# The first layer's MLP of a two-layer transformer block: its first matrix by seven half-size products in seven of eight blocks

## What is computed

```
def squared_relu_mlp(h, w_in, w_out):
    return jnp.square(jax.nn.relu(h @ w_in)) @ w_out
xl = xl + ml[5] * squared_relu_mlp(modulate(xl, norm_mlp_g[i], ml[3], ml[4]), w_mlp_in[i], w_mlp_out[i])
if not last:
    xc = xc + mc[5] * squared_relu_mlp(modulate(xc, norm_mlp_g[i], mc[3], mc[4]), w_mlp_in[i], w_mlp_out[i])
```

## Time and profile before

| | |
|---|---|
| median of 3 runs | 1614.97 us (1614.3 to 1968.04) |
| span of the profiled execution, first to last instruction | 1613.1 us |
| around the span in a run (median less span) | 1.9 us |
| PE busy in the span | 1595.3 us (99%) |
| DVE, POOL, ACT busy | 983.8 us (61%), 618.0 us (38%), 517.5 us (32%) |
| mean granted TensorE clock | 0.998 |

### The profile page before, as it was taken

The page is one execution under the profiler, slowest core; times in us unless marked ns, Lnnn a source line. Parts: engine busy times, 40 slices in busy tenths (PEclk is TensorE's granted clock), DMA queues, the critical chain, the costliest instruction groups (busy, mean ns, idle before and its releaser), DMA issues.

```text
span 1613.1 us, 24225 instructions
## 1 busy us (share of the span) xinstructions
PE 1595.3 (99%) x9440; PEld 1433.7 (89%) x9440; DVE 983.8 (61%) x1315; ACT 517.5 (32%) x931; POOL 618.0 (38%) x402
## 2 busy tenths in 40 slices
PE   8999999999999999999999999999999999999998
PEld 5889988989999999999999888878889888888887
DVE  5697457258756764865784678229975825344364
ACT  4422466233211211211211512138864422222222
POOL 2422565335323322432331544244505644444441
PEclk9999999999999999999999999999999999999999
DMA  9473212213252234223332122110002322323221
GB/s 361 181 284 134 92 41 99 92 66 105 77 185 80 77 122 140 100 95 117 105 112 97 66 91 92 65 56 1 1 1 89 107 93 92 104 91 99 96 79 53
DMA packets 50334, 162.99 MB, mean 101 GB/s; under 512 B 6336, under 2 KB 8768, under 8 KB 46656
## 3 DMA queue, kind: packets, MB, share of 16 engines
q1 hardware_dynamic: 50240, 161.68, 29.1%
HBM read 158.78 MB, written 2.10 MB: 100 GB/s over the span
## 4 chain that ended last, share of the span: by engine, by line
PE 93%; DVE 3%; DMA 2%; issue 1%; ACT 1%; SPq 0%; POOL 0%; POOLq 0%; DVEq 0%; ACTq 0%
PE ps L1714 26%; PE ps L1715 26%; PE ps L1716 26%; PE ps L2259 3%; PE ps L2221 2%; PE ps L2248 1%; PE ps L2126 1%; PE ps L2114 1%; PE ps L2154 1%; PE ps L1938 1%; DMA mod_late<-w_mod_dram 1%; DMA mod_big<-w_mod_dram 1%; DVE h L1315 1%; DMA raw<-units_dram 1%; PE ps L2149 1%
## 5 line engine op out<-in xcount | busy, mean ns | idle before, releaser
L625 POOL TENSOR_TENSOR w_lo<-raw,w_hi 128x1024 fp32r<-128x1024 f32 (+1 forms) x235 | 483.6, 2070 | 837.9 <-ACT w_hi L784 837.7
L1714 PE MATMUL ps<-h,w_hi 128*128 128x384 f32 (+2 forms) x1176 | 409.8, 348 | 1.7 <-DVE h L1315 1.2
L1715 PE MATMUL ps<-h,w_lo 128*128 128x384 f32 (+2 forms) x1176 | 407.6, 347 | 0.0
L1716 PE MATMUL ps<-h,w_hi 128*128 128x384 f32 (+2 forms) x1176 | 407.3, 346 | 0.0
L784 ACT ACTIVATE w_hi<-raw 128x1024 fp32r<-128x1024 f32 x187 | 197.8, 1058 | 372.7 <-PE ps L1716 366.1
L1714 PE MATMUL ps<-hid_lo,w_hi 128*128 128x384 f32 (+2 forms) x800 | 277.6, 347 | 0.0
L1715 PE MATMUL ps<-hid_hi,w_lo 128*128 128x384 f32 (+2 forms) x800 | 276.6, 346 | 0.0
L1716 PE MATMUL ps<-hid_hi,w_hi 128*128 128x384 f32 (+2 forms) x800 | 276.4, 346 | 0.0
L1714 PEld LDWEIGHTS ps<-h,w_hi 128*128 128x128 f32 x1176 | 221.3, 188 | 25.2 <-issue 3.4
L1716 PEld LDWEIGHTS ps<-h,w_hi 128*128 128x128 f32 x1176 | 221.2, 188 | 16.4
L1715 PEld LDWEIGHTS ps<-h,w_lo 128*128 128x128 f32 x1176 | 221.4, 188 | 16.0
(11 more groups left out here) (237 smaller groups left out, 2268.9 us busy)
## 6 DMA issues: line engine op xcount, KB each, us to landing
raw<-units_dram SPq DMA_DIRECT2D x187, 512.0 KB, 3.3
mod_ring<-w_mod_dram SPq DMA_DIRECT2D x96, 256.0 KB, 3.3
mod_big<-w_mod_dram SPq DMA_DIRECT2D x16, 1024.0 KB, 10.2
mod_late<-w_mod_dram SPq DMA_DIRECT2D x8, 1024.0 KB, 7.9
xl<-x_dram SPq DMA_DIRECT2D x2, 2048.0 KB, 8.4
bias<-bias_dram SPq DMA_DIRECT2D x8, 384.0 KB, 3.7
xc<-ctx_dram SPq DMA_DIRECT2D x2, 1024.0 KB, 10.5
out_dram<-out_t SPq DMA_DIRECT2D x16, 128.0 KB, 1.9
```

The lines of the kernel that those rows point to most:

```text
L625: ins = nc.gpsimd.tensor_tensor(w_lo[:, s, sl], raw[:, s, sl], w_hi[:, s, sl].bitcast(F32), op=ALU.subtract)
L1714: mm(out, a[0], b[1], start=start, stop=False)
L1715: mm(out, a[1], b[0], start=False, stop=False)
L1716: return mm(out, a[0], b[0], start=False, stop=stop)
```

## The change

MLP 0 gets 8 blocks of 512 hidden channels. Block 0 takes its first matrix as before (4 units, K of 1024). In blocks 1 to 7 the product of 1024 x 512 weights with 1024 x 768 rows is cut into halves along K, hidden channels and tokens (tokens 0 to 383 are `H0`, 384 to 767 `H1`) and is made of seven products of half size, in Winograd's form, in place of eight. One product is one unit of 24 matmuls with 384 columns. Four sums of weight quarters are made on POOL for each block (`w_sum`, `a21`, `a11`, L764 to L781), and four sums of token halves, which all blocks share, once on DVE (`t1f` to `t4f`, L1664 to L1672), ahead of and between the hidden rows of block 0. Products that belong together are summed in PSUM (`onto`), and between them ACT copies a partial sum of 128x768 to SBUF (`copy`, L979), and DVE adds PSUM to it (`joined`, L1721). Squares and parts are made by quarters of 128x768 (L1649 or L1647 on DVE, L983 on ACT, L1654 on DVE).

The second matrix sums over K of 512 in blocks 0 to 5 (each of their units has two output tiles of 24 matmuls), so the residual additions are made 8 times a block in 6 blocks; the last unit group sums over the 1024 channels of blocks 6 and 7. Units go from 64 to 85, loads stay 64. Modulation chunks move with the blocks: two in blocks 1 to 5, one in blocks 6 and 7; blocks 1 to 4 have a chunk with two instructions a step in the stretch of the products, and one with a single instruction in the stretch of the second matrix. The second layer's MLP stays.

The diff, cut to what is spoken of:

```diff
-STAGES = [("f", 4), ("q0", 4), ("k0", 4), ("dft", 3), ("v0", 4), ("out0", 8), ("mlp0", 64),
+STAGES = [("f", 4), ("q0", 4), ("k0", 4), ("dft", 3), ("v0", 4), ("out0", 8), ("mlp0", 85),
...
+def block_first(b):
+    return 0 if b == 0 else 8 + 11 * (b - 1) if b < 7 else 70
...
+                    def outer_sums():
+                        raw_here(1)
+                        raw_here(3)
+                        if b == 1:
+                            pool.wait_ge(t_lo, 4)
+                        else:
+                            pool.wait_ge(lo_made, M0 + block_first(b - 1) + 4)
+                        nc.gpsimd.tensor_tensor(w_sum[:], a21, a22, op=ALU.add).then_inc(w_sums, 1)
+                        raw_here(0)
+                        pool.wait_ge(w_sums, n + 1)
+                        nc.gpsimd.tensor_tensor(a21, a11, a21, op=ALU.subtract).then_inc(w_sums, 1)
+                    if b < 7:
+                        outer_sums()
+                    low(w)
+                    if b == 7:
+                        outer_sums()
+                    pool.wait_ge(w_sums, n + 2)
+                    pool.wait_ge(lo_made, w + 1)
+                    nc.gpsimd.tensor_tensor(a11, w_sum[:], a11, op=ALU.subtract).then_inc(w_sums, 1)
+                    low(w + 1)
+                    raw_here(2)
+                    pool.wait_ge(w_sums, n + 3)
+                    pool.wait_ge(lo_made, w + 2)
+                    nc.gpsimd.tensor_tensor(w_sum[:], a12, a11, op=ALU.subtract).then_inc(w_sums, 1)
+                    for j in range(2, 11 if b < 6 else 7):
+                        low(w + j)
...
+                def turn_high(j, dst, src):
+                    act.wait_ge(tf_made, (2, 3, 4, 1)[j])
+                    nc.scalar.activation(dst, src, ACT.Copy).then_inc(t_hi, 1)
+                for i in range(4):
+                    u = M0 + i
+                    act.wait_ge(unit_done, u + 1)
+                    for bank, c0, n in both if i < 3 else even:
+                        ins = nc.scalar.activation(hidl_f[:, i, c0:c0 + n], ps[:, 2 * pair_of(u, i, True) + bank, 0:n],
+                                                   ACT.Relu)
+                    ins.then_inc(relu0_made, 1)
+                    high_u(u + 4)
+                    act.wait_ge(sq0_made, i + 1)
+                    nc.scalar.activation(hidh[:, i], hidl_f[:, i], ACT.Copy).then_inc(hq_hi, 1)
+                    if i == 1:
+                        turn_high(0, t3h[:], t3f[:])
+                    elif i == 2:
+                        turn_high(1, t2h[:], t2f[:])
+                        turn_high(2, t4h[:], t4f[:])
+                act.wait_ge(unit_done, M0 + 4)
+                turn_high(3, h_hi[:, 0:4, H1], t1f[:])
...
+                next_block(1)
+                for b in range(1, BLOCKS):
+                    w, n = M0 + block_first(b), 4 * (b - 1)
+                    def copy(side, p, q, func=ACT.Copy):
+                        act.wait_ge(unit_done, w + p + 1)
+                        nc.scalar.activation(quarter(b, q)[2], part_ps(b, side), func).then_inc(s_copied, 1)
+                    def quarter_high(q):
+                        act.wait_ge(sq0_made, 4 * b + q + 1)
+                        nc.scalar.activation(quarter(b, q)[0], quarter(b, q)[2], ACT.Copy).then_inc(hq_hi, 1)
+                    high_sum(b, 3)
+                    copy(0, 0, 2)
+                    high_sum(b, 4)
+                    copy(1, 1, 1)
+                    high_u(w + 5)
+                    copy(0, 2, 0)
+                    high_u(w + 6)
+                    for q in range(4):
+                        if q == 3:
+                            copy(0, 6, 3, ACT.Relu)
+                        if b == 6 and q in (1, 2):
+                            high_sum(7, q)
+                        elif b != 6 or q == 0:
+                            high_u(w + 7 + q)
+                        quarter_high(q)
+                    if b < 6:
+                        next_block(b + 1)
...
+                def square(q, n, src):
+                    if n % 4 == 3 or n < 4:
+                        ins = tt(src, src, src, op=ALU.mult)
+                    else:
+                        ins = V.scalar_tensor_tensor(out=src, in0=src, scalar=0.0, in1=src, op0=ALU.max, op1=ALU.mult)
+                    ins.then_inc(sq0_made, 1)
+                def quarter_low(n, hi, lo, src):
+                    dve.wait_ge(hq_hi, n + 1)
+                    tt(lo, src, hi.bitcast(F32), op=ALU.subtract).then_inc(hq_made, 1)
+                def turn_low(j, lo, src, hi):
+                    dve.wait_ge(t_hi, j + 1)
+                    tt(lo, src, hi.bitcast(F32), op=ALU.subtract).then_inc(t_lo, 1)
...
+                def difference(dst, spare, j0, tok0, j1, tok1):
+                    tt(dst, half_f(j0, 0, tok0), half_f(j1, 0, tok1), op=ALU.subtract).then_inc(dsteps, 1)
+                    st.n = st.n + 1
+                    st.wait(tt(spare, half_f(j0, 1, tok0), half_f(j1, 1, tok1), op=ALU.subtract))
+                    tt(dst, dst, spare, op=ALU.add).then_inc(tf_made, 1)
+                def less(dst, src, n, j, tok):
+                    dve.wait_ge(tf_made, n)
+                    st.wait(tt(dst, half_f(j, 0, tok), src, op=ALU.subtract))
+                    tt(dst, dst, half_f(j, 1, tok), op=ALU.add).then_inc(tf_made, 1)
+                def first_square(i):
+                    dve.wait_ge(relu0_made, i + 1)
+                    square(i, i, hidl_f[:, i])
+                def first_low(i):
+                    quarter_low(i, hidh[:, i], hidl[:, i], hidl_f[:, i])
+                dve.wait_ge(h_made, step(1, 1, KT - 1) + 1)
+                difference(t1f[:], t4f[:], 0, H1, 0, H0)
+                first_square(0)
+                dve.wait_ge(tf_made, 1)
+                difference(t3f[:], t4f[:], 1, H1, 0, H1)
+                first_low(0)
+                less(t2f[:], t1f[:], 1, 1, H1)
+                first_square(1)
+                less(t4f[:], t2f[:], 3, 1, H0)
+                first_low(1)
+                turn_low(0, t3l[:], t3f[:], t3h[:])
+                first_square(2)
+                first_low(2)
+                turn_low(1, t2l[:], t2f[:], t2h[:])
+                turn_low(2, t4l[:], t4f[:], t4h[:])
+                first_square(3)
+                first_low(3)
+                turn_low(3, h_lo[:, 0:4, H1], t1f[:], h_hi[:, 0:4, H1])
+                def add_tile(b, m):
+                    w = M0 + block_first(b) + (7 if b else 4) + m // 2
+                    if m % 2:
+                        dve.wait_ge(unit_done, w + 1)
+                    else:
+                        dve.wait_ge(tile_done, 4 * b + m // 2 + 1)
+                    add_pieces(0, 2 + m % 2, m, 5, xa(0, b, m))
+                def steps(c, ks):
+                    for k in ks:
+                        mod_step(c, k)
+                for m in range(8):
+                    add_tile(0, m)
+                for b in range(1, BLOCKS):
+                    c = MOD_OF[b][0]
+                    def joined(side, p, q):
+                        dve.wait_ge(unit_done, M0 + block_first(b) + p + 1)
+                        dve.wait_ge(s_copied, 4 * (b - 1) + (3, 2, 1)[q])
+                        src = quarter(b, q)[2]
+                        tt(src, part_ps(b, side), src, op=ALU.add).then_inc(s_added, 1)
+                        dve.wait_ge(s_added, 3 * (b - 1) + q + 1)
+                        square(q, 4 * b + q, src)
+                    def low(q):
+                        quarter_low(4 * b + q, *quarter(b, q))
+                    steps(c, range(6))
+                    joined(1, 3, 0)
+                    steps(c, range(6, 7))
+                    low(0)
+                    joined(0, 4, 1)
+                    steps(c, range(7, 8))
+                    low(1)
+                    if b == 6:
+                        extract_late(c, 4)
+                    joined(1, 5, 2)
+                    low(2)
+                    dve.wait_ge(s_copied, 4 * b)
+                    square(3, 4 * b + 3, quarter(b, 3)[2])
+                    low(3)
+                    if b < 6:
+                        add_tile(b, 0)
+                        add_tile(b, 1)
+                        extract_late(c, 0)
+                        for m in range(2, 6):
+                            steps(c + 1, range(2 * m - 4, 2 * m - 2))
+                            add_tile(b, m)
+                        add_tile(b, 6)
+                        extract_late(c + 1, 0)
+                        add_tile(b, 7)
...
+            def first_mlp():
+                first_three(1, M0, [pair_of(M0 + j, j, True) for j in range(3)])
+                pe.wait_ge(relu0_made, 1)
+                unit(M0 + 3, (M0 + 3) % SLOTS, (M0 + 3) % 2, *h_t, even)
+                def second(b, before_tile):
+                    for n in range(4):
+                        u = M0 + block_first(b) + (7 if b else 4) + n
+                        s = u % SLOTS
```

(49 more changed lines are left out.)

405 lines of the change are left out of this document (271 added, 134 removed).

## The result

| | before | after |
|---|---|---|
| median, us | 1614.78 (1614.3 to 1968.04, 4 runs) | 1684.8 (1682.7 to 1684.93, 4 runs) |
| ratio | 1 | 1.0429, 95% interval 1.0414 to 1.0445 |
| span of the profiled execution, us | 1613.1 | 1683.0 |
| TensorE matmuls | 9440 | 9272 |

What follows compares the result with a forecast made beforehand. PE, busy 99% of the span, was taken as the bound. Span 1613.1 - 29.1 (saving) + 26.6 (block 0) + 40 (blocks 1 to 4) + 5 + 8 (last blocks) + 4.5 (clock) = 1668.1, plus 1.9: median 1670.0 us, range 1618 to 1704.

Steps and rivals of the forecast that it cites:

- The saving, -29.1: Blocks 1 to 7: seven products in place of eight save 168 matmuls on PE, 29.1 us.
- 64 instructions become 81 low parts: MLP 0: POOL's 64 instructions become 81 low parts and 28 weight sums, 15 in each block of 512.
- Block 0, +26.6 and 1.7 for the clock: Block 0 after unit 3: PE idles 26.6 us for DVE's ordered work, then loses 1.7 us at half clock.
- the bound was 18.2: Block 0: lower bound of PE's idle time, 18.2 us, if no DVE instruction meets POOL's.
- Blocks 1 to 4, +10 each and 0.7 for the clock: Blocks 1 to 4: PE waits 10 us a block for joined sums and quarters, plus 0.7 us each at half clock.
- Stalls at products 5 and 6: Blocks 1 to 4: PE waits for DVE's first and second `joined`, 1.7 and 0.5 us.
- cost at nothing: Second matrix's stretch, blocks 1 to 4: no loss, as PSUM reads cover DVE; otherwise tile 7 up to 3 us late.
- near 100% busy in the products' stretches: Sign to look for in blocks 1 to 4: DVE near 100% busy during the products.
- The clock, +4.5 in all: Half clock behind PE's waits: 1.7 us in block 0, 0.7 in each of blocks 1 to 4, 4.5 in all.
- Blocks 5 to 7, +13: Last blocks: late quarters cost 5 us in block 5; DVE's backlog from block 6 costs 8 us in block 7.
- DVE keeps up after block 0: Rival for the blocks after block 0: POOL's instructions fall into DVE's waits or PSUM reads, 1617 us; chance 0.21.
- DVE and POOL exclude each other almost wholly: Rival for blocks 1 to 4: hardly any POOL time is hidden, 18 us lost a block, 1702 us; chance 0.10.

Runs made afterwards that it cites:

- run 1: Changed kernel with POOL's low parts and weight sums, and ACT's copies of sums in `w_sum`, cut to 64 of 1024 columns: 1602.6 us.
- run 4: Changed kernel with PE's row sums of modulation chunk 10 moved from block 6 to behind product 1 of block 7: 1684.5 us, ratio 1.0437.
- run 9: Changed kernel with modulation sums in PSUM, block 0 and modulation work reordered, most squares on ACT, late-needed high parts postponed: 1596.9 us, ratio 0.9888.
- run 2: Changed kernel with seven of the eight steps of each late modulation chunk cut to 16 of 512 columns, POOL untouched: 1659.1 us.
- run 5: Changed kernel with the sums of the late modulation chunks kept in PSUM instead of SBUF, POOL's work and DVE's order unchanged: 1647.7 us.

## Why the forecast was right, and where it was off

The mechanism came as forecast: two waits in block 0 (20.25 and 2.97 us), waits for quarters' low parts in blocks 1 to 4, blocks of 75.6 us (74 forecast), and DVE's rows stretched while POOL works. The terms were less exact than their sum.

**The saving, -29.1.** Right: run 1 has blocks of 63.8 us, the counted time of 15 products' worth of matmuls and the row sums. (POOL's "64 instructions become 81 low parts" compares unlike counts: it is 64 and 85, since the page's count rises from 402 to 451, by 21 low parts and 28 sums. The 15 a block, which the sum uses, are right.) A 1536-wide instruction alone took 1.75 to 1.76 us, close to the 1.77 of the rows' slope.

**Block 0, +26.6 and 1.7 for the clock.** Right in size and mechanism: 27.9 together, 24.9 of waiting and 2.9 for the 17 matmuls at half clock behind it. The low part of unit 3 was forecast to end at 419.8 and ended at 418.13 (it starts at 417.17 and takes 0.96). All four of POOL's low parts met DVE, as said. Without meetings the bound was 18.2; run 1 has low part 3 end at 409.83, where PE would have needed it at 393.2, so 16.6 are the order's.

**Blocks 1 to 4, +10 each and 0.7 for the clock.** Measured 11.8 against 10.7. That the sum is so near is partly luck, as errors of both signs cancel. Stalls at products 5 and 6 (1.7 and 0.5) didn't come; quarters 1, 2 and 3 cost 3.0, 0.3 and 2.6 in block 2 (forecast 3.7, 0.7, 3.3). In exchange the second matrix's stretch, which I "cost at nothing", since PSUM reads are over half of it, had waits at tiles: 0.39 and 1.57 us in block 2, 1.85 and 0.63 in block 1. The split before tile 7 was late, as the bound of 3 us had allowed. And half clock adds 1.7 us in block 2 where 0.7 was forecast.

That DVE would be "near 100% busy in the products' stretches" nearly holds: 31.76 of 33.60 us in block 2, though over a whole block it is 64 of 75.7:

```profile
528.40:562.00 33.60, 30.53 (x175) 29.92 (x173) 31.76 (x28) 11.01 (x12) 18.62 (x7) 1.00 0.47 148
```

**The clock, +4.5 in all.** Too small. Counted by their starts, 103 matmuls of the stage run some 0.35 us apart and not 0.173, about 18 us together: 24 in block 0, 27 in block 1, 10 in each of blocks 2 to 4, 9 in block 5, 13 in block 6. Not all of it is lost: block 1, with 27 of them, takes 75.5 us, and block 2, with 10, takes 75.4, so a part only fills time in which PE would have waited for DVE. No run separates the two, and the clock's share of the miss stays open. Windows of 2 us in block 1 and block 2 (PE's busy time and count first, the clock third from the end):

```profile
486.00:488.00 2.00, 1.52 (x5) 1.52 (x6) 1.97 (x3) 0.00 (x0) 0.00 (x0) 0.50 0.59 215
...
562.00:564.00 2.00, 1.99 (x11) 1.99 (x12) 1.78 (x2) 0.15 (x1) 0.00 (x0) 1.00 0.39 152
...
568.00:570.00 2.00, 0.34 (x2) 0.34 (x3) 1.60 (x1) 0.00 (x0) 0.79 (x1) 1.00 0.11 29
570.00:572.00 2.00, 2.00 (x11) 2.00 (x10) 0.99 (x3) 0.00 (x0) 0.00 (x0) 0.78 0.61 234
572.00:574.00 2.00, 2.00 (x8) 2.00 (x7) 0.28 (x1) 0.00 (x0) 1.89 (x1) 0.50 0.03 8
```

The waits for quarter 1 in block 1 and in block 4:

```profile
486.48 0.69 PE L2033 MATMUL ps<-hidl,w_hi 128*128 128x384 f32 x1 [3.00 <-DVE hidl L1654]
...
713.30 0.45 PE L2033 MATMUL ps<-hidl,w_hi 128*128 128x384 f32 x1 [2.98 <-DVE hidl L1654]
```

Behind the wait of 3.00 us in block 1 PE runs at once at 1.2 GHz, for 17 matmuls; behind the one of 2.98 in block 4 it does so from 714.5 on, for 10; behind the one of 3.00 in block 2 it does not, and the stretch comes at 571.2, behind a third wait, of 2.59. So the same wait did and did not bring it. The rule of the Trainium skill that the forecast had weighed beside it ("TensorE: Matmul & The Clock Gate", section "Why this matters for your kernels": an idle gap of some length puts the array back on half clock) agrees in so far as each stretch of blocks 1 to 6 begins within 1.6 us behind a wait, but it doesn't tell blocks 1 and 2 apart. Its sum, 8.5, would have been nearer to the 18 us counted than the 4.5 taken, and both lie below it.

**Blocks 5 to 7, +13.** This term was the furthest off: 7.9 in block 5 (forecast 5), 13.4 in block 6, 2.1 in block 7, 23.4 in all. "Block 6 has no second matrix behind it, so DVE carries its backlog of about 10 us into block 7" was priced at 8 us. The backlog had the right size (the wait is 10.74), but it came due inside block 6, at the row sums of chunk 10. I had listed the waits that products and quarters have on DVE and passed over these sums, which stand in PE's order behind product 5 and need DVE's split. Yet their place isn't what made the term too small: in run 4 they are out of the way, the backlog comes due in block 7 as forecast, and the same time is lost. What was wrong is the price, 8 us for blocks 6 and 7 where 15.5 were lost in either order.

**The rivals.** "DVE keeps up after block 0" (1617) asked that meetings fall into waits; they didn't, but run 9 nearly reaches that state in blocks 1 to 7, by making it so. "DVE and POOL exclude each other almost wholly" (1702) was too dark. By term, the forecast's miss of 14.8 us is blocks 5 to 7, +10.4, blocks 1 to 4, +4.4, and block 0, -0.4; clock included.

## What to carry to other kernels

Price an instruction on DVE by its memory as well as its width: with both inputs in SBUF it costs its own time plus what is left of POOL's instruction (so does a CAST or TENSOR_SCALAR from SBUF to SBUF), with one in PSUM its own time. Before work is moved onto a shared order, list every PE instruction that waits for that engine, small side jobs too; whether moving one of them helps needs a run, since the wait may only move (run 4). And where a change saves PE work but loses time, first take POOL's work away in a trial: if the blocks fall to the count of columns, the saving may be had, as here, by moving operands into PSUM or work to ACT.

## What was not expected of the hardware

- A CAST and a TENSOR_SCALAR with one input in SBUF are held up by POOL too. I had written of two-input instructions only. DVE and then POOL in block 6:

```profile
857.51 2.34 DVE L1414 CAST acc_hi<-mod_acc 128x512 fp32r<-128x512 f32 x1
859.89 2.74 DVE L1415 TENSOR_TENSOR acc_lo<-mod_acc,acc_hi 128x512 fp32r<-128x512 f32 x1
```

```profile
856.78 2.78 POOL L725 TENSOR_TENSOR w_lo<-w_sum,w_hi 128x1024 fp32r<-128x1024 f32 x1
859.74 2.34 POOL L781 TENSOR_TENSOR w_sum<-raw 128x1024 f32<-128x1024 f32 x1 [0.17 <-POOL w_lo L725]
```

  The same CAST took 0.43 us alone, in run 2. The Trainium skill's page "SBUF — State Buffer", in the section named above, counts casts and `tensor_scalar` among the operations that can take the shared ports, by a fast mode with two of them; by that rule, the rows agree.
- With its sum in PSUM the first step of a chunk, a TENSOR_SCALAR, takes 0.74 to 0.76 us (mean 0.747 over 14, in run 5), where from SBUF to SBUF its mean was 1.57: slower than at its best (0.48 on average in run 1, where POOL hardly works), faster beside POOL.
- POOL pays too. In block 0 of run 9 three of its 1024-wide instructions take 3.9 us each, for 2.40 alone, beside DVE's 1536-wide ones, of which the first came before them.
